# Expert matmuls in column groups of 32, 64 or 128 instead of 32 alone

## The reference

```python
for e in range(N_EXPERTS):
    h = jax.nn.silu(x @ w_gate[e]) * (x @ w_up[e])
    y = y + (h @ w_down[e]).astype(x.dtype) * combine[..., e:e + 1]
```

## Time and profile before

| | us |
|---|---|
| median of 3 runs | 1209.92 |
| lowest and highest run | 1206.95, 1216.91 |
| profiled execution, its own time | 1205.93 |
| its span | 1204.1 |
| TensorE busy | 1110.6 (92%) |
| VectorE, ScalarE, GpSimd busy | 566.9, 260.6, 220.4 |
| mean granted TensorE clock | 0.97 |

### The profile page before, as it was taken

How to read it: one execution, slowest core, us unless ns; L and a number is a source line. 1 busy time by engine, 2 the same in 40 slices (tenths; PEclk the granted TensorE clock), 3 DMA queues, 4 the chain that set the end, 5 groups by cost and what they waited for, 6 DMA issues and landing times.

```text
span 1204.1 us, 18616 instructions
## 1 busy us (share of the span) xinstructions
PE 1110.6 (92%) x7460; PEld 623.9 (52%) x7466; DVE 566.9 (47%) x1351; ACT 260.6 (22%) x615; POOL 220.4 (18%) x383
## 2 busy tenths in 40 slices
PE   8998999999899969999979989999999978999995
PEld 4556776654674543333335547787784553333331
DVE  2068779710563354553457331350452354555337
ACT  0214355321440001111111222332330001111114
POOL 0015545430201211000124310000000111100123
PEclk9999999999899989999999999999999989999998
DMA  9103403253635178899787222001205167899854
GB/s 364 71 1 117 182 1 141 71 176 130 33 85 214 64 276 290 338 415 382 268 274 267 81 109 70 1 1 70 70 18 228 64 274 253 322 414 376 308 190 156
DMA packets 41976, 215.58 MB, mean 179 GB/s; under 512 B 4504, under 2 KB 6104, under 8 KB 32544
## 3 DMA queue, kind: packets, MB, share of 16 engines
q1 hardware_dynamic: 24288, 152.76, 32.8%
q0 software_dynamic: 17312, 60.80, 16.2%
q10 hardware_dynamic: 288, 0.80, 0.2%
HBM read 181.02 MB, written 33.29 MB: 178 GB/s over the span
## 4 chain that ended last, share of the span: by engine, by line
PE 78%; DVE 9%; DMA 5%; issue 4%; ACT 2%; POOL 2%; SPq 0%; DVEq 0%; POOLq 0%; ACTq 0%
PE pair L1542 13%; PE pair L1146 9%; PE pair L1426 9%; PE pair L1563 7%; PE pair L1267 5%; PE pair L1672 5%; PE pair L1345 5%; PE pair L1157 4%; PE pair L1390 3%; PE pair L1134 2%; PE pair L1528 2%; DMA arena<-x_rows,ints 2%; DMA ring<-in_even_w_in 2%; PE pair L1705 2%; PE pair L1129 1%
## 5 line engine op out<-in xcount | busy, mean ns | idle before, releaser
L1542 PE MATMUL pair<-ring,arena 128*32 128x512 f32 x608 | 128.5, 595 | 0.0
L1146 PE MATMUL pair<-ring,xT 128*128 128x512 f32 x256 | 111.3, 593 | 0.6 <-DMA ring<-in_even_w_in 0.6
L1542 PE MATMUL pair<-arena 128*32 128x512 f32 x640 | 86.4, 601 | 12.4 <-issue 8.7
L1267 PE MATMUL pair<-xT,ring 128*128 128x296 f32 x320 | 85.1, 421 | 6.9 <-ACT arena L1789 3.0
L918 POOL TENSOR_TENSOR arena<-arena 128x128 f32<-128x128 f32 x140 | 58.4, 451 | 144.9 <-PE pair L1193 78.1
L896 POOL TENSOR_SCALAR small<-small 128x1 f32<-128x1 f32 (+3 forms) x45 | 15.5, 344 | 367.3 <-DVE small L2347 317.0
L1146 PEld LDWEIGHTS pair<-ring,xT 128*128 128x128 f32 x256 | 48.1, 190 | 59.5 <-issue 57.9
L1345 PE MATMUL pair<-arena 128*128 128x264 f32 (+8 forms) x270 | 74.7, 407 | 2.8 <-ACT arena L1779 1.8
L1563 PE MATMUL pair<-ring,arena 128*32 128x512 f32 x368 | 75.4, 611 | 1.5 <-issue 1.1
L1042 POOL DMA_INDIRECT arena<-x_rows,ints x26 | 26.5, 1019 | 262.7 <-PE pair L1528 162.6
L1267 PEld LDWEIGHTS pair<-xT,ring 128*128 128x128 f32 x320 | 60.4, 193 | 25.8 <-issue 9.4
(11 more groups left out here) (388 smaller groups left out, 2048.3 us busy)
## 6 DMA issues: line engine op xcount, KB each, us to landing
ring<-in_moe_w_gate_up SPq DMA_DIRECT2D x14, 2048.0 KB, 9.9
arena<-in_moe_w_gate_up SPq DMA_DIRECT2D x12, 2048.0 KB, 11.0
ring<-in_moe_w_down SPq DMA_DIRECT2D x14, 1024.0 KB, 11.7
y_rows<-arena SPq DMA_DIRECT2D x25, 512.0 KB, 8.6
arena<-in_moe_w_down SPq DMA_DIRECT2D x12, 1024.0 KB, 9.8
xT<-in_moe_w_gate_up SPq DMA_DIRECT2D x6, 2048.0 KB, 14.2
ring<-in_even_w_in SPq DMA_DIRECT2D x5, 2048.0 KB, 7.8
y_rows<-xr POOLq DMA_DIRECT2D x13, 512.0 KB, 9.0
```

The source lines that it names most:

```text
L1146: last = pe.matmul(ps[0:P, 0:n], xT[:, k, 128 * i:128 * i + P], w[:, k, :], start=(k == 0), stop=(k == chunks - 1))
L1267: last = pe.matmul(ps[0:w.shape[2], 512 * s:512 * s + n], w[:, k, :], xT[:, k, n * s:n * s + n], start=(k == 0), stop=(k == KD - 1))
L1542: last = pe.matmul(bank[c, :], xgT[:, e % 2, k, c], expert_place(x)[0][:, k, :], start=(k == 0), stop=(k == KD - 1))
```

## The change

A table `COLUMNS` is made of `BLOCKS`: where all four runs of a block belong to one expert, they become one group of 128 columns; where runs 0 and 1, or 2 and 3, belong to one expert they become one group of 64; a run that is left stays a group of 32. `gate_up` and `down` loop over these groups, and `last_gate_up` uses all 128 columns at once.

```diff
+def column_groups(blocks):
+    out, j = [], 0
+    while j < 4:
+        n = 4 if blocks == [blocks[0]] * 4 else 2 if j % 2 == 0 and blocks[j] == blocks[j + 1] else 1
+        out.append((32 * j, 32 * n, blocks[j]))
+        j += n
+    return out
+
+COLUMNS = [column_groups(b) for b in BLOCKS]
...
                 for k in range(KD):
-                    for j, x in enumerate(BLOCKS[e]):
-                        c = slice(32 * j, 32 * j + 32)
+                    for lo, n, x in COLUMNS[e]:
+                        c = slice(lo, lo + n)
                         last = pe.matmul(bank[c, :], xgT[:, e % 2, k, c], expert_place(x)[0][:, k, :],
                                          start=(k == 0), stop=(k == KD - 1))
...
                     for k in range(2):
-                        for j, x in enumerate(BLOCKS[e]):
-                            c = 32 * j
-                            last = pe.matmul(psum[2][c:c + 32, 512 * half:512 * half + 512],
-                                             hT[:, e % 2, 128 * k + c:128 * k + c + 32],
+                        for c, n, x in COLUMNS[e]:
+                            last = pe.matmul(psum[2][c:c + n, 512 * half:512 * half + 512],
+                                             hT[:, e % 2, 128 * k + c:128 * k + c + n],
                                              expert_place(x)[1][:, k, 512 * half:512 * half + 512],
                                              start=(k == 0), stop=(k == 1))
...
                     for k in range(KD):
-                        for j in range(4):
-                            c = slice(32 * j, 32 * j + 32)
-                            last = pe.matmul(psum[1][c, 512 * n:512 * n + 256], xgT[:, x % 2, k, c], expert_place(OWN)[0][:, k, half],
-                                             start=(k == 0), stop=(k == KD - 1))
+                        last = pe.matmul(psum[1][:, 512 * n:512 * n + 256], xgT[:, x % 2, k, :], expert_place(OWN)[0][:, k, half],
+                                         start=(k == 0), stop=(k == KD - 1))
                     last.then_inc(gu_ps.sem, 1)
```

## The result

The changed kernel takes 1365.88 us (median of 4 runs, 1364.21 to 1372.64) where the kernel before takes 1213.41 us (4 runs, 1206.95 to 1220.6): a ratio of 1.1266, 95% interval 1.1227 to 1.1305. It is 152 us slower. The profiled execution took 1366.4 us, its span 1364.6 us, against 1205.9 and 1204.1 us before.

A forecast was written before the change was run, and what follows sets the result against it. TensorE was taken to bound the kernel, busy for 92% of the span. 1205.9 us plus 186.4 for lost overlap and width changes, less 19.2 of waits, gave 1373.1, taken as a median of 1375 us, range 1335 to 1415.

The forecast's parts named there:

- Waves: Expert matmuls: equal-width groups run side by side at 0.429 us a wave, so wider groups remove records, not waves.
- the even blocks: Blocks with two groups of 64 or one of 128 columns: costed at nothing.
- Lost overlap, 144.2 us: Seven mixed blocks: 64- and 32-column groups don't overlap, 0.859 us more in each of 84 steps per layer.
- The rival that unlike widths run side by side: Steps of the seven mixed blocks: groups on disjoint columns overlap, so nothing is lost; 1205 us, chance 9%.
- Changes of width, 0.138 us each: Mixed blocks and their boundaries: each change empties the array; 153 per layer, 21.1 us a layer.
- A mixed `gate_up`: `gate_up` in blocks with 64- and 32-column groups: about 15.8 us, against 6.9 us unmixed.
- the price into 64 columns: Switching the array into 64-column width: 0.146 us, against about 0.13 us into 32 columns.
- Waits off, 19.2 us: TensorE's longer work hides waits: 4.3 and 4.4 us at the gather, 8.65 us "issue" pieces, 1.9 us low clock.
- the gather's: Wait before block 3: longer `down(0)` covers it and its low clock, 4.3 us off in layer 0, 4.4 in layer 1.
- the "issue" pieces: Idle before `gate_up(5)` and `gate_up(9)`, read as waits for down weights of experts 7 and 12: 8.65 us off.
- an allowance for a median above its profiled execution: Whole kernel: the profiled execution was 4.0 us under the median, so 1373.1 us was raised to 1375 us.

The follow-up runs named there:

- e1: Changed kernel with only the mixed-width blocks put back to four groups of 32: 1205.98 us, ratio 0.9939 to the kernel before; repeated, 1204.52 us, 0.9945.
- e2: Changed kernel with widths outermost: in a mixed block all steps of one width, then all of the other: 1322.52 us, ratio 1.0912 to the kernel before.
- e3: Changed kernel with layer 1's blocks as two groups of 64 (except own-expert gate and up), leaving out one expert's matmul in seven blocks: 1290.43 us.
- e7: Kernel before, with layer 1's down weights of experts 7 and 12 loaded for only 16 of 1024 columns: 1207.79 us, ratio 0.9953.
- e5: Changed kernel with `down` put back to four groups of 32: 1328.67 us, ratio 1.0964 to the kernel before.
- e6: Changed kernel with `gate_up` and the last block's gate and up put back to four groups of 32: 1253.84 us, ratio 1.0310 to the kernel before.
- e8: Kernel before, with second gate/up loads behind down weights and slot indices of blocks 3 and 4 earlier: 1191.21 us, ratio 0.9797; repeated, 1193.46 us, 0.9855.
- e11: Changed kernel with each block's groups in reverse order in `down`: 1375.61 us, ratio 1.1354 to the kernel before.
- e9: Kernel before, with the second of two freed experts' gate and up weights issued behind the down weights of experts 7 and 12: 1203.17 us, ratio 0.9890.
- e10: Kernel before with both reorderings of e8 and the group table of e1: 1190.63 us, ratio 0.9836.

## Why the prediction was right

Predicted 1375 us, range 1335 to 1415; measured 1365.88 us.

**Waves.** Right: one, two or four groups of one width take 0.429 us a wave (7.0 to 7.1 us for 16, 32 and 64 records in e1), so widening brings nothing, and the even blocks cost nothing.

**Lost overlap, 144.2 us.** Right, and the larger term: e2 takes nearly all changes of width away and is still 9.1% slower; e3 takes the unlike widths away from one layer and that layer's loss is gone. The rival that unlike widths run side by side falls.

**Changes of width, 0.138 us each.** Right: 0.134 us from e2, and a step of 1.98 us where the terms gave 1.99. A mixed `gate_up` of 15.8 and `down` of 7.9 us were foretold; 15.9 and 7.9 came. For the price into 64 columns there was some luck: it was read from L1213, which follows L1212 in the same width and another height, so that a change of width costs as much was assumed and not seen.

**Waits off, 19.2 us.** Right in place and cause: in the changed trace all are absent but 0.3 us of the gather's; e7 shows the weights behind the "issue" pieces, e5 and e6 that a wait goes just where the longer step lies between its cause and its end, and the stretches of the changed kernel come out with them taken off (below). What they are worth in the kernel before is known only roughly: e8 and its repeat give 25 and 18 us by medians (0.9797 and 0.9855), 16.9 and 11.7 us by the stretches of their profiled executions, where 19 were forecast.

**What the sum lacked.** It was 6.7 us too high against the profiled execution (1373.1 against 1366.4). The term is an overlap across the boundary of `down` and the next `gate_up`: where both have the same width there, on other columns, two waves run together. The timeline of the changed kernel at `down(3)` and `gate_up(5)`:

```profile
547.94 1.17 PE L1575 MATMUL pair<-mixT,arena 128*32 128x512 f32 x2
548.47 0.64 PE L1555 MATMUL pair<-arena 128*64 128x512 f32 x1
548.94 0.59 PE L1575 MATMUL pair<-mixT,arena 128*64 128x512 f32 x1
548.95 1.14 PE L1555 MATMUL pair<-arena 128*64 128x512 f32 x2
```

`gate_up(5)` begins on columns 0 to 63 while `down(3)` still streams its group of 64 on the others (the first line merges a 32-column record with the first of these). At four places per layer, 0.86 us each, that is 6.9 us, and with it the stretches come out at 160.4 + 93.2 - 7.7 - 3.4 = 242.5 and 164.4 + 93.2 - 11.5 - 3.4 = 242.7 us, measured 242.2 in both. e11 takes the overlap away and the stretches grow by 7.3 us where 7.4 was worked out. I had counted that those entries need no change of width, and not that equal width also lets them start early. The other 2 us between 1375 and 1373.1 were an allowance for a median above its profiled execution; the changed kernel's median is 0.6 us below.

**Left open.** e1 is 0.5 to 0.6% faster than the kernel before, twice. Its profiled executions don't show where: its stretches are 161.5 us in both layers (repeated run) against 160.4 and 164.4. One thing differs across the executions: in four kernels whose last `down` or `gate_up` is in groups of 32 (e5, e7, e8, e9) TensorE had one idle piece of 3.3 to 4.8 us at the matmul of the own rows that follows the last block; the changed kernel and e10 had none and e1 0.5 us at most, but neither had e6 more than 0.5 us nor the profiled execution of the kernel before any. No experiment was made on it.

## What to carry to other kernels

Before widening column groups, look at the pace: if four narrow groups already stream in the time of one, there are only records to save. Groups shared the array here only while their width was the same (64 beside 32 columns, float32, 512 moving columns), so give each run of matmuls one width, and take the narrow one for all where a block needs it once; if widths must mix, put them outermost, which here left 9% of loss in place of 13%. And price a slowdown with the waits that it hides, which here gave back a tenth of it and pointed to two reorderings that make the kernel before 1.5 to 2% faster.

## What the runs showed of the hardware that I had not expected

Matmuls of different code lines overlap as well as those of one loop, if width is equal and the columns differ: two waves at each boundary in the changed kernel, about four in e2, never the whole of the eight that were there. It saves time only where the second group's columns would else stand empty (e6 against the changed kernel). Why it stops at four wasn't tried; the copied rows that `gate_up(5)` of e2 waits for were there 4.5 us before its first matmul, at 534.69 against 539.22 us, so it isn't they. Two records of one float32 matmul on a group stay in order, 0.43 us apart (0.48 us right behind a change into 64 columns), while the other group's go on beside them.
